# The last sum over weight blocks, in the second layer, on GpSimd instead of VectorE

## The reference, cut to what matters

```python
def odd_layer(x, norm_g, w_in, b_forget, w_out):
    hn = rmsnorm(x, norm_g)
    proj = hn @ w_in
    q, k, v, z, f_logit = jnp.split(proj, cuts, axis=-1)
    log_f = jax.nn.log_sigmoid((f_logit + b_forget).astype(jnp.float32))
    o = forgetting_attention(q.reshape(shp), k.reshape(shp), v.reshape(shp), log_f)
    o = o * jax.nn.silu(z)
    return x + o @ w_out
...
    cum = jnp.cumsum(log_f, axis=1).transpose(0, 2, 1)
...
        s = jnp.einsum('bhqd,bkhd->bhqk', qi, k).astype(jnp.float32) * scale
        s = s + cqi[..., None] - cum[:, :, None, :]
        s = jnp.where(kpos[None, :] <= qpos[:, None], s, -jnp.inf)
        p = jax.nn.softmax(s, axis=-1).astype(v.dtype)
        return jnp.einsum('bhqk,bkhd->bqhd', p, v)
```

## Time and profile before

| | us |
|---|---|
| median of 3 runs | 2652.45 |
| lowest and highest | 2652.05, 2652.7 |
| span of the profiled execution | 2651.5 |
| TensorE busy in the span | 2628.4 |
| VectorE busy | 1674.4 |
| ScalarE busy | 581.2 |
| GpSimd busy | 316.9 |

### The profile page before, as it was taken

The page is one execution under the profiler, slowest core; times in us unless marked ns, Lnnn a source line. Parts: engine busy times, 40 slices in busy tenths (PEclk is TensorE's granted clock), DMA queues, the critical chain, the costliest instruction groups (busy, mean ns, idle before and its releaser), DMA issues.

```text
span 2651.5 us, 54568 instructions
## 1 busy us (share of the span) xinstructions
PE 2628.4 (99%) x20666; PEld 2513.0 (95%) x20666; DVE 1674.4 (63%) x3637; ACT 581.2 (22%) x1413; POOL 316.9 (12%) x479
## 2 busy tenths in 40 slices
PE   8999999999999999999999999999999999999998
PEld 7888888999999999999999999999999999999998
DVE  7666667565556556777676653656555565788855
ACT  3222221110001112232222230122211012434411
POOL 0011010010001000133333320112210000000000
PEclk9999999999999999999999999999999999999999
DMA  6444332544444444444343335333434444444543
GB/s 248 140 143 142 135 135 99 188 141 163 162 162 166 159 149 168 146 140 138 131 142 127 127 111 200 143 128 137 150 140 146 160 164 161 182 167 150 190 159 111
DMA packets 63761, 401.08 MB, mean 151 GB/s; under 512 B 6816, under 2 KB 13488, under 8 KB 17456
## 3 DMA queue, kind: packets, MB, share of 16 engines
q1 hardware_dynamic: 62992, 397.62, 42.2%
q0 software_dynamic: 672, 2.11, 0.5%
HBM read 397.60 MB, written 2.11 MB: 151 GB/s over the span
## 4 chain that ended last, share of the span: by engine, by line
PE 96%; DVE 2%; issue 1%; POOL 0%; ACT 0%; DVEq 0%; DMA 0%; SPq 0%; ACTq 0%; POOLq 0%
PE psum L591 59%; PE psum L535 16%; PE psum L544 6%; PE psum L859 2%; PE psum L1065 1%; PE psum L764 1%; PE psum L566 1%; PE psum L672 1%; PE psum L1074 1%; PE psum L688 1%; PE psum L698 1%; PE psum L968 1%; PE psum L828 1%; PE psum L1026 1%; PE psum L665 0%
## 5 line engine op out<-in xcount | busy, mean ns | idle before, releaser
L591 PE MATMUL psum<-h,ring 128*128 128x128 f32 x4384 | 524.1, 275 | 0.0
L591 PEld LDWEIGHTS psum<-h,ring 128*128 128x128 f32 x4384 | 507.8, 192 | 1.1 <-issue 0.2
L591 PE MATMUL psum<-mix,ring 128*128 128x128 f32 x3994 | 477.7, 275 | 0.4
L591 PEld LDWEIGHTS psum<-mix,ring 128*128 128x128 f32 x3994 | 461.4, 192 | 1.4 <-DVE near L1696 1.3
L535 PE MATMUL psum<-h,ring 128*128 128x256 f32 x2016 | 451.6, 381 | 0.0
L535 PEld LDWEIGHTS psum<-h,ring 128*128 128x128 f32 x2016 | 377.0, 190 | 60.9 <-issue 12.7
L1703 DVE TENSOR_TENSOR near<-psum,near 128x128 f32<-128x128 f32 x128 | 37.2, 291 | 343.2 <-PE psum L591 343.2
L544 PE MATMUL psum<-ring,h 128*128 128x128 f32 x1536 | 175.5, 275 | 0.0
L544 PEld LDWEIGHTS psum<-ring,h 128*128 128x128 f32 x1536 | 174.1, 192 | 0.6 <-DVE h L1628 0.2
L1663 DVE TENSOR_TENSOR ring<-ring 128x1024 f32<-128x1024 f32 x112 | 138.0, 1232 | 0.0
L591 PE MATMUL psum<-ring 128*128 128x128 f32 x1024 | 124.9, 275 | 0.6 <-DVE near L1696 0.6
(11 more groups left out here) (468 smaller groups left out, 3870.8 us busy)
## 6 DMA issues: line engine op xcount, KB each, us to landing
ring<-w_out SPq DMA_DIRECT2D x80, 1024.0 KB, 5.2
ring<-w_odd SPq DMA_DIRECT2D x64, 1024.0 KB, 5.0
ring<-w_hgrn SPq DMA_DIRECT2D x64, 1024.0 KB, 4.9
ring<-w_even SPq DMA_DIRECT2D x48, 1024.0 KB, 4.9
ring<-w_nsa SPq DMA_DIRECT2D x48, 1024.0 KB, 6.2
ring<-w_rg SPq DMA_DIRECT2D x40, 1024.0 KB, 5.8
ring<-w_cmp_in SPq DMA_DIRECT2D x8, 1024.0 KB, 4.9
ring<-w_rgg SPq DMA_DIRECT2D x10, 512.0 KB, 7.5
```

The source lines that it names most:

```text
L591: mm = pe.matmul(dst, stationary, moving, start=new and j == 0, stop=new and j == kh - 1, skip_group_check=not new)
```

## The change

GpSimd gets a function `last_form`, which makes t4 of one pair, with the same inc of `forms_made`. GpSimd calls it inside its loop over turns, behind `masks(i)` and the issue of the next broadcast: for pairs 1, 2 and 3 of turn i and pair 0 of turn i + 1. VectorE no longer calls `fourth_form` for the pairs of this layer (31 calls), and `three_forms` now also waits until the t4 before has been made, since both bump the same semaphore. The first `fourth_form` of the output projection behind the layer (`fast2`) stays on VectorE.

```diff
+            def last_form(i, q):
+
+                n = fast_odd.number(i, q)
+                g.wait_ge(forms_made, after(2 * n + 1))
+                g.wait_ge(used, done(odd1, i, 7 * q - 1))
+                (b11, b21, b12, b22), (t2, t1, t4) = pieces(fast_odd, q)[0]
+                g.tensor_tensor(t4, b21, t2, ALU.subtract).then_inc(forms_made, 1)
+
             with g.Fori(0, TWO_HEADS - 1) as i:
                 masks(i)
                 g.wait_ge(ck_ready, after(4 * i + 4))
                 g.dma_start(cum_two, rows[ds(i + 1, 1)].to_broadcast([P, 2, T])).then_inc(cum_in, 16)
+                for q in (1, 2, 3):
+                    last_form(i, q)
+                last_form(i + 1, 0)
             masks(TWO_HEADS - 1)
+            for q in (1, 2, 3):
+                last_form(TWO_HEADS - 1, q)
...
                         v.wait_ge(landed[f.ph.loads[n].slot], f.ph.loads[n].land0 + i * f.ph.loads[n].land_per)
+                if f is fast_odd or f is fast2:
+                    v.wait_ge(forms_made, after(2 * f.number(i, q)))
...
                 copied.then_inc(later_read if e else first_read, 5 if e else 2)
-            fourth_form(fast_odd, 0, 1)
             v.wait_ge(f_ln, after(1))
...
                     fifth_sum(fast_odd, i, 0, q_two)
-                    fourth_form(fast_odd, i, 1)
...
                 fifth_sum(fast_odd, i, 1, k_two)
-                fourth_form(fast_odd, i, 2)
...
                 fifth_sum(fast_odd, i, 2, v_two)
-                fourth_form(fast_odd, i, 3)
...
                 if last:
                     fourth_form(fast2, 0, 0)
-                else:
-                    fourth_form(fast_odd, i + 1, 0)
```

## The result

The changed kernel takes 2671.25 us (median of 4 runs, 2670.47 to 2671.88) against 2652.39 us for the kernel before: 1.0071 times as long, 95% interval 1.0056 to 1.0085, 18.9 us more. The forecast was 2668.4, with 2660 to 2676 as its range.

What follows compares the result with a forecast made beforehand. TensorE, busy 99% of the span, was taken as the bound. Start 7.2, clock 2.7, pair 3 6.9 and seams -0.9 summed to +15.9 us, giving 2668.4 against 2652.45, range 2660 to 2676.

Steps and rivals of the forecast that it cites:

- The start: Layer's start, turn 0's pair 1: t4 stands behind GpSimd's broadcast and masks, so TensorE's run 6 idles 7.2 us.
- The clock: Behind the idle gap at the layer's start: TensorE's clock halves; bounded by nothing and 5.4 us, middle +2.7 taken.
- 1.6 us into it: End of the profile: the clock falls from 2.4 to 1.2 GHz 1.6 us into a stretch with little TensorE work.
- Pair 3: t4 made after pair 2 holds up VectorE's normalisation, so pair 3's run 3 starts late: 6.9 us over eight turns.
- at 694.57 and holds until 696.77: Pair 2 of a steady turn: GpSimd's t4 starts at 694.57 and, at 2.2 us, holds VectorE's normalisation until 696.77.
- The seams: Between turns, pair 0's run 4: relieved VectorE against moved masks; half the 1.7 us gain over five seams, -0.9 us.
- The steady pairs 0 and 1: Steady turns: t4 takes 2.2 us while VectorE only reads PSUM, well before TensorE's run 6; nothing lost.
- (a): Rival: the normalisation gets past GpSimd, t4 hidden in every turn, only the start is paid: +9.0, 2661.5 us; 12%.
- (b): Rival: the clock stays low for the whole pair behind the gap: +12.5 instead of 2.7, 2678.2 us; 8%.
- (c): Rival: GpSimd's chain is no bound at the start, the normalisation passes and VectorE's relief remains: -1.7, 2650.8 us; 2%.
- (d): Rival: the broadcast lands several us sooner, the clock holds and the normalisation passes: about +3 to +5 us; 2%.

Runs made afterwards that it cites:

- the t4 ahead of the chain: Changed kernel with turn 0 written out and its pair 1 t4 on GpSimd, called before GpSimd's wait for the cumulative sums: 2661.39 us.
- both moves: Changed kernel with the first t4 before GpSimd's wait for the cumulative sums and pair 3's t4 behind the normalisation, all 31 on GpSimd: 2651.8 us.

## Why the prediction was right

All four terms of the sum are there, at the places named, and no other in the layer; it came out 3 us low, and that is sizes. They measure 7.55 + 2.95 + 9.2 - 1.4 = 18.3 us.

**The start**, 7.2 forecast: 7.55. GpSimd's chain is the one of the earlier trace rows, but its first landing took 0.32 us longer (1.80 against 1.48 us of idle time), and t4 took 2.35 instead of 2.2 us. In return, run 6 started 0.05 us behind t4, not 0.16. That the queue and not the engine is the cause is shown by the t4 ahead of the chain, which removes all of it.

**The clock**, 2.7 taken as the middle of a bound: 2.95 (6.53 - 3.58). In three other kernels with gaps of 7.5 to 8.1 us it was 1.6, 2.5 and 2.9, so it varies at much the same gap; that the middle of the bound came close is luck. That it hangs on the gap is shown by the three kernels without one, where PEclk stays 1.00. The fall "1.6 us into it" of the prediction counts from the edge of a window; from 2638.6 on TensorE had only two short matmuls left, so this was no measure of how soon the clock falls in a gap. In the changed kernel PEclk was still 1.00 from 570 to 572.

**Pair 3**, 6.9 forecast: 9.2, the one term that was clearly too small. Its mechanism is shown by three kernels: without t4 there, with t4 behind the normalisation, and in halves. In a loop turn run 3's wait went from 0.11 to 1.32 us (1.22 to its start, and its own 2.05 instead of 1.95), where 1.02 was worked out. The difference of 0.3 has three parts: t4's 0.15; GpSimd starts 0.16 after L1681's end, not 0.09; and the added wait delays `three_forms` by 0.11, which the prediction had priced at nothing without saying so. VectorE's sequence behind t4 took as long as forecast (0.35, then 0.85). The step that was mis-sized is "at 694.57 and holds until 696.77".
The Trainium skill's rule in "SBUF — State Buffer", section Who interferes with whom, that the hold lasts for a whole instruction, agrees with the trace: 2.289 us for a multiplication of 0.286. The 4497 ns that the Trainium skill gives for 2048 columns ("GPSIMD Engine Reference", section 3.1), halved as an estimate to 2.25, was nearer to the measured 2.35 than the 2.2 taken.

**The seams**, -0.9 as half of a gain of 1.7: -1.4. The wait went from 0.34 to 0.05. The first mask add follows t4 at once, without a loop's turn between. The masks do meet L2086, but it hits only the tail of a 128-column add, at a cost of 0.11 us (0.80 instead of 0.69), and the last add, of 256 columns, waits for it (1.08 us instead of 0.64) and not the other way.

**The steady pairs 0 and 1**, nothing forecast: nothing found. t4 stands beside reads of PSUM and delays none: L1735 at 692.16 takes its plain 0.29 us inside a t4 that runs from 691.27 to 693.62.

**The rivals.** (a), the normalisation getting past GpSimd, is refuted by L1830's 2.289 us at most. (b), a clock that stays low over a whole pair: it came back before the second run behind the gap had ended. (c) and (d) needed a GpSimd chain that is some us shorter; its waits were 1.80 and 4.38 us.

## What to carry to other kernels

Work moved to an idle engine is not free where that engine's queue is in order: look at what stands ahead of it there, DMA landings too, and put the moved work ahead of the waits it doesn't depend on. And look at what runs on the other engine while it runs: here a 2.35 us instruction off the critical path held a multiplication of 0.3 us that was on it. When 99% of the time is one engine's, relieving another is worth at most the waits for it, here 1.4 us of 2652 (2.1 with both moves), and can cost ten times that.

## What the runs showed of the hardware

A GpSimd addition or subtraction of float32 took 0.40 us for 128 columns, 0.63 for 256, 1.27 for 512 and 2.35 for 1024; the last two grow by 0.27 us per 128 columns, more than the 0.23 between the first two, from which the forecast had drawn its line. Another 256-column addition of this kernel took 0.73; why, no run shows.

The added wait, always met already, cost VectorE 0.11 to 0.15 us inside the loop over turns (0.44 us from L1720's start to L1677's in turn 2, 0.29 in the kernel before; 0.29 behind the maxima against 0.18). In the turns written out it cost 0.01 us there and 0.07 behind the maxima. That the loop's worked-out value is the reason was not tested by itself.

A VectorE read of PSUM with its other input in SBUF was not held by GpSimd (0.29 us inside a t4). A multiplication from SBUF to SBUF was, for the whole instruction (2.289 us instead of 0.286).

TensorE's granted clock fell to 0.50 in a gap of 4.2 us as in gaps of 7.5 to 8.1, and was still 0.50 through nearly all of the first run behind it. Over five kernels the price was 1.6 to 2.95 us; the 4.2 us gap cost 2.7, within the 1.6 to 2.95 of the longer ones.
